# Block inverse of a two-block model: the transposed factor of each level made by TensorE and fetched in one copy

## The reference, cut to what matters

```python
c = GDN_CHUNK                      # 64 tokens
a_mat = beta[..., :, None] * jnp.einsum('nhcid,nhcjd->nhcij', k, k) * d_strict
rhs = jnp.concatenate([beta[..., None] * v, (beta * gam)[..., None] * k], axis=-1)
sol = lax.linalg.triangular_solve(a_mat, rhs, left_side=True, lower=True, unit_diagonal=True)
u0, w = sol[..., :dv], sol[..., dv:]
```

## Time and profile before

| what | value |
|---|---|
| median of three runs (lowest, highest) | 1992.57 us (1991.77, 1993.93) |
| the profiled execution's own time | 1989.61 us |
| its span, first to last instruction | 1987.8 us |
| mean granted TensorE clock | 0.957 of full |
| TensorE busy | 1702.6 us (86%), 17970 matmuls |
| VectorE busy | 835.2 us (42%) |
| ScalarE busy | 638.2 us (32%) |
| GpSimd busy | 242.3 us (12%) |

### The profile page before, as it was taken

How to read it: one execution, slowest core, us unless ns; L and a number is a source line. 1 busy time by engine, 2 the same in 40 slices (tenths; PEclk the granted TensorE clock), 3 DMA queues, 4 the chain that set the end, 5 groups by cost and what they waited for, 6 DMA issues and landing times.

```text
span 1987.8 us, 44255 instructions
## 1 busy us (share of the span) xinstructions
PE 1702.6 (86%) x17970; PEld 962.9 (48%) x17970; DVE 835.2 (42%) x1522; ACT 638.2 (32%) x1218; POOL 242.3 (12%) x270
## 2 busy tenths in 40 slices
PE   5998895987778777897889779999998797799996
PEld 2444543544444444444655664354446655663452
DVE  1567524111111112376655753151357647543331
ACT  3414611000000000335534535252245426523442
POOL 0002211111111111005112100000002103000001
PEclk8998996999999999998999799999998999999998
DMA  9759015999999999611000003110211000013101
GB/s 359 262 190 301 1 50 222 367 422 425 425 425 424 424 424 422 256 65 42 4 3 2 3 4 126 43 43 32 80 43 34 4 2 2 4 65 105 43 1 42
DMA packets 75099, 307.76 MB, mean 155 GB/s; under 512 B 10908, under 2 KB 22300, under 8 KB 57888
## 3 DMA queue, kind: packets, MB, share of 16 engines
q1 hardware_dynamic: 63280, 291.98, 37.4%
q0 software_dynamic: 5360, 9.33, 1.3%
q10 hardware_dynamic: 6272, 3.81, 0.7%
HBM read 301.01 MB, written 16.52 MB: 160 GB/s over the span
## 4 chain that ended last, share of the span: by engine, by line
PE 73%; DVE 10%; another core or an unknown queue 6%; ACT 5%; issue 4%; ACTq 1%; DMA 1%; DVEq 0%; POOL 0%; POOLq 0%
PE bank L522 12%; PE bank L2323 12%; PE bank L2339 6%; PE bank L1066 6%; PE bank L572 4%; PE bank L2161 3%; PE bank L2245 3%; PE bank L1037 2%; PE bank L565 2%; PE bank L538 2%; DVE arena L1645 1%; PE bank L2185 1%; PE bank L2173 1%; ACT arena L1078 1%
## 5 line engine op out<-in xcount | busy, mean ns | idle before, releaser
L522 PE MATMUL bank<-hT,arena 128*128 128x512 f32 (+1 forms) x640 | 287.2, 604 | 3.8 <-ACTq L1079 2.4
L2323 PE MATMUL bank<-arena 128*64 128x256 f32 x1792 | 214.5, 396 | 68.4 <-remote 68.4
L2323 PEld LDWEIGHTS bank<-arena 128*64 128x64 f32 x1792 | 133.9, 142 | 159.1 <-issue 108.6
L522 PEld LDWEIGHTS bank<-hT,arena 128*128 128x128 f32 (+1 forms) x640 | 122.4, 193 | 161.4 <-issue 156.9
L2929 DVE COPY arena<-bank 128x256 f32<-128x256 f32 x32 | 13.6, 425 | 329.6 <-PE bank L2331 329.6
L2339 PE MATMUL bank<-arena 128*64 128x512 f32 x448 | 104.0, 607 | 16.3 <-remote 16.3
L2583 ACT ACTIVATE arena<-bank 128x512 f32<-128x512 f32 x32 | 19.1, 597 | 292.8 <-PE bank L2339 292.8
L1078 ACT ACTIVATE arena<-bank 128x512 f32<-128x512 f32 (+2 forms) x124 | 73.2, 590 | 117.4 <-PE bank L522 79.0
L1066 PE MATMUL bank<-arena 128*128 128x512 f32 x256 | 110.4, 593 | 0.0
L572 PE MATMUL bank<-hT,arena 128*128 128x512 f32 x224 | 106.7, 615 | 2.2 <-remote 2.2
L554 PE MATMUL bank<-arena 64*64 64x64 f32 x3200 | 75.8, 237 | 32.8 <-DVE arena L1645 15.0
(11 more groups left out here) (454 smaller groups left out, 2881.2 us busy)
## 6 DMA issues: line engine op xcount, KB each, us to landing
arena<-w_gate SPq DMA_DIRECT2D x28, 2048.0 KB, 30.5
arena<-w_up SPq DMA_DIRECT2D x28, 2048.0 KB, 21.0
arena<-w_down SPq DMA_DIRECT2D x28, 2048.0 KB, 26.3
arena<-w_ada SPq DMA_DIRECT2D x12, 2048.0 KB, 20.0
arena<-w_in SPq DMA_DIRECT2D x10, 2048.0 KB, 10.1
arena<-w_out SPq DMA_DIRECT2D x6, 2048.0 KB, 8.0
arena<-w_in SPq DMA_DIRECT2D x6, 1536.0 KB, 7.2
hT<-w_up SPq DMA_DIRECT2D x4, 2048.0 KB, 20.9
```

The costliest lines, as they stand in the source:

```text
L522: m = pe.matmul(bank[b][0:w, :], slot2(n)[:, k, c:c + w], hT[:, k, :], start=(k == 0), stop=(k == KD - 1))
L2323: mm = pe.matmul(bank[b][c * CAP:(c + 1) * CAP, 0:FE // 2], XT[j][:, k % 4, k // 4, :], e_slot(e_at(e, i), KD)[:, k, c * (FE // 2):(c + 1) ...
```

## The change

TensorE makes Y itself. In front of each `across` a new function `turned` writes the transposed 16 blocks of T to PSUM: the blocks bound for partitions 0 to 63 by `pe.transpose`, those for 64 to 127 by a product with the identity. At level 1 it writes to columns 256 to 511 of the banks that `across` uses, later to banks 4 to 7. ScalarE fetches them with one copy per direction (`turned_moved`: the whole 128x512 at level 1, later the 256 columns that the level before renewed), in front of `product_moved`. The two copies of the far half, `y_far`, and VectorE's transposes after each merge are gone. At the last level VectorE transposes T into the tile of the matrix (free once both `across` of that level are done, `g_v_done`), and the last merge goes there; u and w read it from there. The waits that protect banks 4 to 7 move to level 2, in front of `turned`.

```diff
+            def turned(d, b, at, T):
+
+                T = placed(T)
+                for s in range(2):
+                    for h in range(2):
+                        cols = slice(at + (2 * s + h) * CG, at + (2 * s + h + 1) * CG)
+                        for f, g in quarters_of:
+                            o, t, one = bank[b + f][half(g), cols], T[half(f), g, s, h], ident[half(f), half(f)]
+                            m = pe.transpose(o, t, one) if g == 0 else pe.matmul(o, t, one, start=True, stop=True)
+                m.then_inc(sem(f"g_y_done{d}"), 1)
             def back(d, Y, V, last):
...
-                            y = Y[half(g), g, s, h] if f == g else y_far[d][half(g), cols]
-                            v = V[half(g), f, s, h]
+                            y, v = Y[half(g), f, s, h], V[half(g), f, s, h]
...
                 for ht in range(3):
                     if ht > 0:
-                        kk_free.wait()
                         keys_products(ht)
...
+                            if l == 2 and d == 0:
+                                for n in gam_full:
+                                    n.wait()
+                            if l == 2 and d == 1:
+                                kk_free.wait()
+                            turned(d, 2 * d if l == 1 else 4 + 2 * d, 256 if l == 1 else 0, g_T[d])
                             across(d, g_Bn[d], g_T[d]).then_inc(sem(f"g_v_done{d}"), 1)
                         for d in range(2):
-                            far_full[d].wait(2)
+                            y_full[d].wait()
                             v_full[d].wait()
                             back(d, g_Y[d], g_V[d], l == LEVELS - 1).then_inc(sem(f"g_t_done{d}"), 1)
                     for d in range(2):
-                        y_full[d].wait(LEVELS)
+                        y_full[d].wait()
...
-                                m = pe.matmul(o[half(f), s, t], block_of(g_Y[d], f, s, t), g_vtok[half(f), t, h * GD:(h + 1) * GD],
+                                m = pe.matmul(o[half(f), s, t], block_of(g_Bn[d], f, s, t), g_vtok[half(f), t, h * GD:(h + 1) * GD],
...
-            def changed_half(d, Y, l):
-
-                for g in range(2):
-                    dst, src = y_far[d][half(g)], Y[half(1 - g), 256 * g:256 * g + 256]
-                    if l > 0:
-                        dst, src = renewed(dst, l, 1 - d), renewed(src, l, 1 - d)
-                    act.activation(dst, src, ACT.Copy).then_inc(sem(f"y_far_full{d}"), 1)
+            def turned_moved(d, Y, l):
+
+                b, at = (2 * d, 256) if l == 1 else (4 + 2 * d, 0)
+                dst, src = two(Y), banks[:, b:b + 2, at:at + 256]
+                if l > 1:
+                    dst, src = renewed(dst, l - 1, 1 - d), renewed(src, l - 1, 1 - d)
+                act.activation(dst, src, ACT.Copy).then_inc(sem(f"g_y_full{d}"), 1)
...
-                    for d in range(2):
-                        y_full[d].wait()
-                        changed_half(d, g_Y[d], 0)
                     if ht > 0:
                         raw((6, 2)[ht - 1], 2)
                     for l in range(1, LEVELS):
                         for d in range(2):
+                            y_done[d].wait()
+                            if l == 1:
+                                v_done[d].wait()
+                            turned_moved(d, g_Y[d], l)
                             if l > 1:
-                                y_full[d].wait()
-                                changed_half(d, g_Y[d], l - 1)
-                            v_done[d].wait()
+                                v_done[d].wait()
                             if l == 1:
                                 pt_full[d].wait()
                             product_moved(d, g_V[d], l, -1.0)
...
                     for l in range(1, LEVELS):
                         for d in range(2):
-                            t_done[d].wait()
                             if l < LEVELS - 1:
+                                t_done[d].wait()
                                 take_over(d, g_T[d], l, False).then_inc(sem(f"g_t_full{d}"), 1)
-                                n_t[d] += 1
-                                dve.wait_ge(sem(f"g_t_full{d}"), n_t[d])
-                                dve.transpose(g_Y[d], g_T[d]).then_inc(sem(f"g_y_full{d}"), 1)
                             else:
-                                take_over(d, g_Y[d], l, True).then_inc(sem(f"g_y_full{d}"), 1)
+                                v_done[d].wait(LEVELS - 1)
+                                chain(dve.transpose(g_Bn[d], g_T[d]))
+                        if l == LEVELS - 1:
+                            for d in range(2):
+                                t_done[d].wait()
+                                take_over(d, g_Bn[d], l, True).then_inc(sem(f"g_y_full{d}"), 1)
```

More of the change, by code:

```diff
@@ L770, in rwkv_chunks @@
                             t_full[d].wait()
+                            if l == 2 and d == 0 and ct == 1:
+                                k_free.wait()
+                            if l == 2 and d == 0 and ct == 0:
+                                pe.wait_ge(sem("r_k_free"), 2)
+                            turned(d, 2 * d if l == 1 else 4 + 2 * d, 256 if l == 1 else 0, r_bt[:, ct, d])
                             across(d, r_Bn[d], r_bt[:, ct, d]).then_inc(sem(f"g_v_done{d}"), 1)
                         for d in range(2):
-                            far_full[d].wait(2)
+                            y_full[d].wait()
                             v_full[d].wait()
                             back(d, r_kmt[:, ct, d], r_kr[:, ct, d, 0], l == LEVELS - 1).then_inc(sem(f"g_t_done{d}"), 1)
-                    if ct == 1:
-                        k_free.wait()
-                    else:
-                        pe.wait_ge(sem("r_k_free"), 2)
                     for d in range(2):
-                        y_full[d].wait(LEVELS)
+                        y_full[d].wait()
                         o = pieces(bank[2 * d])
@@ L1207, in act_second @@
                             value_tile(j)
-                v_done, u_done, pt_full, y_full = [[Count(act, sem(f"{n}{d}")) for d in range(2)] for n in
-                                                   ("g_v_done", "g_u_done", "g_pt_full", "g_y_full")]
+                v_done, u_done, pt_full, y_done = [[Count(act, sem(f"{n}{d}")) for d in range(2)] for n in
+                                                   ("g_v_done", "g_u_done", "g_pt_full", "g_y_done")]
                 w_done = Count(act, sem("g_w_done"))
@@ L1232, in act_second @@
                             product_moved(d, g_V[d], l, -1.0)
-                    for n in y_full:
-                        n.n += 1
                     if ht == 0:
@@ L1284, in act_second @@
                 args_full, k_done, w_done = Count(act, sem("r_args_full")), Count(act, sem("r_k_done")), Count(act, sem("g_w_done"))
-                v_done, u_done, y_full = [[Count(act, sem(f"{n}{d}")) for d in range(2)] for n in ("g_v_done", "g_u_done", "g_y_full")]
+                v_done, u_done, y_done = [[Count(act, sem(f"{n}{d}")) for d in range(2)] for n in ("g_v_done", "g_u_done", "g_y_done")]
                 def decays(ct, d):
@@ L1341, in act_second @@
                                        ACT.Copy).then_inc(sem(f"g_uw_free{d}"), 1)
-                for n in v_done + u_done + [w_done, args_full]:
+                for n in v_done + y_done + u_done + [w_done, args_full]:
                     n.clear()
@@ L1736, in dve_second @@
                     Count(dve, sem(n)) for n in ("r_sw_full", "r_func_full", "r_km_full", "r_k_done", "r_bn_full", "r_tok_full")]
-                t_done = [Count(dve, sem(f"g_t_done{d}")) for d in range(2)]
-                n_t = [0, 0]
+                t_done, v_done = [[Count(dve, sem(f"{n}{d}")) for d in range(2)] for n in ("g_t_done", "g_v_done")]
                 def chunks8(ap):
```

59 lines of the change are left out of this document (27 added, 32 removed).

## The result

| what | before | after |
|---|---|---|
| median, both on one chip (lowest, highest) | 1992.17 us (1987.48, 1993.93) | 2133.24 us (2124.19, 2135.19) |
| ratio, 95% interval | | 1.0703 [1.0667, 1.074] |
| span | 1987.8 us | 2129.8 us |
| mean granted TensorE clock | 0.957 | 0.952 |

The changed kernel is slower by 141 us. The forecast had the direction, and 50 of the 141; 2133 lies far outside 2024 to 2063.

A forecast was written before the change was run, and what follows sets the result against it. The prediction took TensorE's instruction supply, close to the engine chain, to bound the inverse: +67.5 us for added blocks, 17 absorbed, other terms 0, so +50.5 on the 1992.6 us median; forecast 2042 us, range 2024 to 2063.

The forecast's parts named there:

- As arithmetic that is little: ... 15 ns a pair, 0.36 us a call: In `turned`: the added 24 instruction pairs need only 15 ns each of TensorE's issue time, 0.36 us a call.
- the forecast 50.5: Whole kernel: net slowdown in us, 67.5 for added instruction blocks less 17 absorbed.
- the absorbed time: In the ten inverses: time where supply wasn't the limit takes up 17 us of the added cost; bounds 0 and 26.
- The supply in blocks of 256: In the inverse: TensorE's instructions arrive in blocks of 256, one per 3.45 to 4.0 us; 18.75 blocks are added.
- the stops of 0.5 us: Sign of being right, in GDN inverses: TensorE stops 0.5 us or more at every block, counted as "issue".
- the 67.5 us: In the inverses: gross cost of 18.75 added instruction blocks at 3.6 us each, if nothing absorbs it; 65 to 75.
- The free time: In the ten inverses: 26 us not limited by supply, most in the two first RWKV inverses, about 1 each in eight others.
- The removals at nothing: VectorE's transposes and ScalarE's half copies taken out of the levels: gain 0 where instruction supply decides.
- The first level, the last level and the moved waits at nothing: In each inverse: whole-matrix copy 0 or +4 us, late VectorE transpose 0 to +3, waits 0; each taken as 0.
- (a): Rival for the levels: the engine chain limits, not supply; a level falls to about 2.9 us, total 1975 us; 9%.
- (b): Rival for the inverse: the clock falls because TensorE idles more between blocks; +35, 2077 us; 6%.
- (c): Rival in `turned`: 64-row transposes don't issue as one pair, 1600 more instructions; +22, 2065 us; 3%.

The follow-up runs named there:

- extra: The kernel before, with 12 of the 16 products of `across` issued twice in every call and no transposes added: 2034.96 us, ratio 1.021.
- grouped: The changed kernel with `turned` reordered: all 8 transposes first, then all 8 identity products, same instruction count: 2038.82 us, one run.
- products: The changed kernel with all 16 blocks of `turned` made by identity products, no transposes, 32 more instructions a level: 2056.25 us, ratio 1.0321.
- alternate: The changed kernel with transpose and product strictly in turn inside `turned`, 16 changes of kind a call instead of 10: 2450.02 us, one run.
- one_turn: The kernel before, with a single 64x64 transpose, result unused, in the middle of each `across` call: 1991.16 us, ratio 0.9996.

## Why the prediction was right in direction and wrong in size

**The failed step** is the sentence "As arithmetic that is little: ... 15 ns a pair, 0.36 us a call". The 15 ns came from `back`, in which only products stand; the transposes of the earlier trace rows stand in a group of their own. A price was carried from one mixture of instructions to another, and it was given no upper bound. The measured term is 1.92 us a call. With it TensorE's level is 2 x 1.92 + 2 x 0.62 + 0.69 + 0.47 + 0.13 = 6.4 us, where the prediction took the supply's 3.6 x 352/256 = 4.95 as the longer. The difference, 1.45 us over 50 levels, is 72 us; with the 19 of the clock and the forecast 50.5 that makes 142, and 141 were measured. That it fits so closely is partly chance: the absorbed time was mis-sized too, as told next, and the 19 us aren't all new, since the kernel before had granted clocks of 0.62 to 0.84 in four of its own ten windows.

**The supply in blocks of 256** was right, and its net price came out 5 to 8 us below the forecast: extra, which adds just these instructions, came to +43, grouped to +46, where +50.5 was forecast. In the changed kernel itself it is hidden, so the stops of 0.5 us, the levels of 4.7 to 5.3 us and the windows of 24 to 26 us weren't there. The gross figures were less exact. A block in the dense stretch of products took 3.3 to 4.0 us from stop to stop (986.71, 989.97, 993.93, 997.78), near the 3.45 to 4.0 taken, but extra's +42.7 means that some 25 of the 67.5 us are absorbed, near the bound of 26 and not the 17 chosen. The free time had also been put in the wrong places. The prediction says that most of the 26 us lies in the two first RWKV inverses. These windows of the view of the earlier trace rows, the first GDN inverse and the first RWKV inverse of the second layer, aren't among the lines that it went by:

```profile
1502.00:1524.40 22.40, 16.62 (x665) 14.93 (x662) 15.22 (x26) 11.96 (x33) 0.00 (x0) 0.77 0.22 74
...
1676.00:1698.60 22.60, 16.00 (x613) 14.11 (x615) 18.44 (x32) 13.48 (x36) 0.00 (x0) 0.78 0.01 4
```

Above 18.1 us the first RWKV inverses have 5.3 and 4.5 us, 9.8 together, and the first GDN inverses, at 22.90 and 22.40, have 9.1, where the prediction counted about 1 each. In extra 44.6 of the 45.8 us by which the span grew lie between merges; the first levels, with 3.75 of the 18.75 blocks (13.5 us at 3.6), cost 1.2 us. The sum has a slip besides: 1992.6 + 50.5 is 2043, not 2042.

**The removals at nothing** fit: grouped has them and extra hasn't, and grouped is 4 us slower, not faster; it ran once.

**The first level, the last level and the moved waits at nothing**: right for grouped, whose span grew by 49.2 us, 45.8 of it between merges; 3.4 us is left, in the range of 0 to 7 that was given. Extra, which has none of the three, has 1.2 there, so that some 2 us remain for them. In the changed kernel 23 us lie outside the merges' windows. Two calls of `turned` at 1.92 us stand there in each inverse too, ten times 3.84 or 38; what offsets 15 of them stays open.

**The rivals.** (a), the chain alone: fell with extra and products. (b), the clock: partly true, 19 us in four inverses here, and the whole inverse at 0.50 in alternate. Why it falls in those four and not in the GDN ones, which issue the same TensorE instructions between merges, stays open. The rival was priced as a matter of TensorE idling, but TensorE was busy for over 97% of the time in each of those four windows. (c) fell: 2400 pairs for 100 calls. No rival had TensorE's own time in it, though "an engine that becomes the bound" is the first thing to ask of added work.

## What to carry to other kernels

Price added instructions by a row with the same neighbours, not only the same shape: each switch between 64x64 float32 transposes and products cost 0.15 to 0.17 us here, so they belong in one group if they are needed at all. Where an inner loop of small matmuls is already at the rate at which instructions arrive, work moved to TensorE costs by its instruction count, and what it frees on other engines gained nothing here. To see which of the two limits holds, add instructions that are known to be cheap (extra) and compare with the change.

## What the hardware showed that was not expected

- Float32 transposes in 64x64 quarters overlap with each other (in grouped two start every 0.055 us) but not with products: 0.15 to 0.17 us at each change, either way, beside 0.055 to 0.058 between such passes.
- Two 128-row products in succession in the same column half of the array: 0.109 us a pass; in the two halves in turn two passes per 0.102. Changing from 64-row to 128-row products took 0.15 to 0.16 us, and back 0.20.
- Instruction packets of TensorE never started less than 3.17 us apart in these twelve traces, and its stops for want of instructions came every 256 instructions.
- TensorE's added time and its wait for instructions don't simply add up: 0.32 us more a call (one_turn) left the time at 0.9996 [0.9977, 1.0016], though single inverses moved up and down.
- The granted clock went to 0.50, the 1.2 GHz level, with TensorE busy all the time, where transposes and products took turns one by one (alternate); with the same instructions in groups (grouped) it was 1.00 in all ten windows from merge to merge.
